# Moving x updates, norm transposes and the first weight unit around the stage boundaries of a two-block transformer kernel

## What is computed

```
x = x + gt_m * (merged @ w_out)                                  # stage out1
x = x + gt_f * swiglu(norm(x)*(1+sc)+sh, w_gate_up, w_down)      # f0
x = x + 0.5 * swiglu(rmsnorm(x), ...)                            # f1
x = x + short_conv(rmsnorm(x), conv_w_in, conv_w, conv_w_out)    # cv, cb, co
x = x + 0.5 * swiglu(rmsnorm(x), ...)                            # f2
shared = kv(rmsnorm(x, kv_norm))                                 # kv
x = x + 0.5 * swiglu(rmsnorm(x), ...)                            # f3
cmp = compress(shared k, v)                                      # xp, cm
x = x + nsa(rmsnorm(x), ...)                                     # qg, gn, nsa, wo
x = x + 0.5 * swiglu(rmsnorm(x), ...)                            # f4
swiglu(h, wgu, wd) = (silu(h @ wg) * (h @ wu)) @ wd              # d_ff 2816
rmsnorm(x, g) = x * rsqrt(mean(x*x) + eps) * g
```

## Time and profile before

| | |
|---|---|
| median of 3 runs | 1701.11 us (1697.21 to 1703.31) |
| profiled execution, own time | 1702.62 us |
| its span in the trace | 1700.8 us |
| PE busy | 1510.3 us, 89% of the span |
| DVE busy | 843.8 us, 50% |
| ACT busy | 690.7 us, 41% |
| share of PE in the chain that ended last | 78% |
| of DVE, ACT, DMA, issue | 9%, 5%, 4%, 3% |

### The profile page before, as it was taken

How to read it: one execution, slowest core, us unless ns; L and a number is a source line. 1 busy time by engine, 2 the same in 40 slices (tenths; PEclk the granted TensorE clock), 3 DMA queues, 4 the chain that set the end, 5 groups by cost and what they waited for, 6 DMA issues and landing times.

```text
span 1700.8 us, 17940 instructions
## 1 busy us (share of the span) xinstructions
PE 1510.3 (89%) x6942; PEld 1203.1 (71%) x6942; DVE 843.8 (50%) x1011; ACT 690.7 (41%) x864; POOL 36.1 (2%) x52
## 2 busy tenths in 40 slices
PE   5979886769998999989889999889997777889998
PEld 2757674658887788867668887668886664568886
DVE  1465572544545454444745545445445346544453
ACT  2334343234343444444344444633433445444342
POOL 0010000000000000000000000100000010000000
PEclk8899997879999999999999999989999777999999
DMA  8654553535565456544545564535555230045562
GB/s 297 204 189 133 198 186 112 173 99 184 187 193 173 153 174 197 178 145 148 173 146 182 191 190 156 160 99 192 185 186 173 79 124 1 4 145 187 185 193 78
DMA packets 187879, 270.10 MB, mean 159 GB/s; under 512 B 8350, under 2 KB 134118, under 8 KB 187816
## 3 DMA queue, kind: packets, MB, share of 16 engines
q1 hardware_dynamic: 186660, 267.08, 48.1%
q10 hardware_dynamic: 996, 1.88, 0.3%
q0 software_dynamic: 160, 0.26, 0.1%
HBM read 268.15 MB, written 1.05 MB: 158 GB/s over the span
## 4 chain that ended last, share of the span: by engine, by line
PE 78%; DVE 9%; ACT 5%; DMA 4%; issue 3%; SPq 0%; POOL 0%; ACTq 0%; DVEq 0%
PE bank L1525 23%; PE bank L1527 23%; PE bank L1526 23%; DVE w_lo_ring L1091 2%; ACT w_hi_ring L797 2%; DMA raw_ring<-in_w_in_dram 2%; PE bank L1549 2%; PE bank L1651 1%; DMA arena<-in_w_mod_dram 1%; PE bank L1619 1%; PE bank L1704 1%; DMA raw_ring<-in_w_br_moba_dram 1%; DVE arena L1376 1%; PE bank L1780 1%; DVE arena L1360 0%
## 5 line engine op out<-in xcount | busy, mean ns | idle before, releaser
L1091 DVE TENSOR_TENSOR w_lo_ring<-raw_ring,w_hi_ring 128x2048 fp32r<-128x2048 f32 (+1 forms) x231 | 525.3, 2277 | 563.1 <-ACT w_hi_ring L1043 371.5
L1525 PE MATMUL bank<-w_hi_ring,h_hi 128*128 128x512 f32 (+2 forms) x1392 | 562.4, 404 | 3.2 <-issue 3.2
L1526 PE MATMUL bank<-w_lo_ring,h_hi 128*128 128x512 f32 (+2 forms) x1392 | 549.6, 395 | 0.0
L1527 PE MATMUL bank<-w_hi_ring,h_lo 128*128 128x512 f32 (+2 forms) x1392 | 549.0, 394 | 0.0
L1043 ACT ACTIVATE w_hi_ring<-raw_ring 128x2048 fp32r<-128x2048 f32 x162 | 310.0, 1916 | 343.4 <-PE bank L1527 343.4
L1525 PEld LDWEIGHTS bank<-w_hi_ring,h_hi 128*128 128x128 f32 x1392 | 271.1, 195 | 65.9 <-issue 13.3
L1527 PEld LDWEIGHTS bank<-w_hi_ring,h_lo 128*128 128x128 f32 x1392 | 269.5, 194 | 56.9
L1526 PEld LDWEIGHTS bank<-w_lo_ring,h_hi 128*128 128x128 f32 x1392 | 270.9, 195 | 51.6
L797 ACT ACTIVATE w_hi_ring<-raw_ring 128x2048 fp32r<-128x2048 f32 (+1 forms) x69 | 128.9, 1875 | 186.5 <-PE bank L1527 118.4
L1525 PE MATMUL bank<-w_hi_ring,f_hi 128*128 128x512 f32 x440 | 171.6, 390 | 7.5 <-DVE f_lo L1484 7.5
L1527 PE MATMUL bank<-w_hi_ring,f_lo 128*128 128x512 f32 x440 | 171.4, 389 | 0.0
(11 more groups left out here) (228 smaller groups left out, 900.2 us busy)
## 6 DMA issues: line engine op xcount, KB each, us to landing
raw_ring<-in_ffn_w_gate_up_dram SPq DMA_DIRECT2D x176, 512.0 KB
raw_ring<-in_ffn_w_down_dram SPq DMA_DIRECT2D x44, 1024.0 KB
raw_ring<-in_w_in_dram SPq DMA_DIRECT2D x22, 1024.0 KB
raw_ring<-in_w_gate_up_dram SPq DMA_DIRECT2D x44, 512.0 KB
raw_ring<-in_w_mod_dram SPq DMA_DIRECT2D x18, 1024.0 KB
raw_ring<-in_w_down_dram SPq DMA_DIRECT2D x11, 1024.0 KB
raw_ring<-in_conv_w_in_dram SPq DMA_DIRECT2D x16, 512.0 KB
arena<-in_w_mod_dram SPq DMA_DIRECT2D x6, 1024.0 KB, 15.3
```

Of the source, the lines that this page charges most:

```text
L1091: dve.tensor_tensor(w_lo[:, u % RING, 0:words], raw[:, r % RING, 0:words], w_hi[:, u % RING, 0:words].bitcast(F32), ALU.subtract).then_inc ...
L1525: pe.matmul(dst, hi, whi, start=start, stop=False)
L1526: pe.matmul(dst, hi, wlo, start=False, stop=False)
L1527: return pe.matmul(dst, lo, whi, start=False, stop=stop)
```

## The change

The change touches six places. I call them by the stages on both sides: f0/f1, f1/cv, co/f2, f2/kv, wo/f4 and f3/xp.

1. In a feed-forward's last step the splits of n1 are issued before the transposed activations are read out, and the low split of n2 after the x updates. The high split of n3 goes behind the next norm's squares. This holds for f0 to f3.
2. The last down product becomes four items `dn`, one for each quarter, and at f0/f1, f1/cv and f2/kv the transposes of groups 0 and 1 stand ahead of the last quarter.
3. The last unit of co and wo is done by row half (`by_tt`), with its own semaphore `half_done`, and groups 0 and 1 stand between the halves.
4. n1 is cut in two: its first two row blocks (`gu`, sub 0, or the first part of kv) stand ahead of groups 2 and 3, and the other two behind them and `square`.

Beginning and end of the other norms (1, 6 and 7) stay.

```diff
+    def ffn(f, stage, norm, then=None, begun=False):
+        body = add("ffn", f=f, stage=stage, norm=norm, unit=len(units) - (2 if begun else 0), begun=begun)
...
+        for q in range(4):
+            if q == 3 and then:
+                plan.extend(tgroup("norm", 2, norm=then))
+            add("dn", of=body, q=q)
+    def norm_rest(n):
+        plan.extend(tgroup("norm", 4, norm=n)[2:])
+        add("square")
+    def begin_glu(stage, norm):
+        u = len(units)
+        units.extend([(stage, 0, 0), (stage, 0, 1)])
+        add("gu", unit=u, sub=0)
+        norm_rest(norm)
+        add("gu", unit=u, sub=1)
+    def lin_out(stage, then):
+        lin(stage, 0, 2)
+        add("lin", stage=stage, chunk=1, part=0, parts=2, unit=len(units))
...
+        add("lin", stage=stage, chunk=1, part=1, parts=2, unit=u, sub=0, subs=2, by_tt=True)
+        add("evac", stage=stage, chunk=1, tt=0)
+        plan.extend(tgroup("norm", 2, norm=then))
+        add("lin", stage=stage, chunk=1, part=1, parts=2, unit=u, sub=1, subs=2, by_tt=True)
+        add("evac", stage=stage, chunk=1, tt=1)
+        add("then split", unit=u)
...
-    ffn(0, "f0", 1)
-    norm(2, True)
-    ffn(1, "f1", 2)
-    norm(3, True)
+    ffn(0, "f0", 1, then=2)
+    begin_glu("f1", 2)
+    ffn(1, "f1", 2, then=3, begun=True)
+    begin_glu("cv", 3)
...
-    for c in range(2):
-        lin("co", c, 2)
-    norm(4, True)
-    ffn(2, "f2", 4)
-    norm(5, True)
-    for c in range(3):
+    lin_out("co", 4)
+    begin_glu("f2", 4)
+    ffn(2, "f2", 4, then=5, begun=True)
+    part("kv", 0, 0, 2, inside=[tgroup("norm", 4, norm=5)[2:] + [dict(kind="square")], []])
+    part("kv", 0, 1, 2)
+    plan.extend(evac("kv", 0))
+    for c in range(1, 3):
...
-    for c in range(2):
-        lin("wo", c, 2)
-    norm(8, True)
-    ffn(4, "f4", 8)
+    lin_out("wo", 8)
+    begin_glu("f4", 8)
+    ffn(4, "f4", 8, begun=True)
...
# ACT, item loop
+                if k in ("square", "xp") and after_norm:
+                    u = after_norm.pop()
+                    split(u, unit_raw[u], u - RING + 1)
# ACT, ffn step
+                        for q in qs[1:] if jb < NJ - 1 else [1]:
+                            next_split(q)
...
+                        if jb == NJ - 1:
+                            next_split(2)
...
+                    u = item["unit"] + 3 * NJ - 1 + RING
+                    if u < len(units):
+                        after_norm.append(u)
# DVE, ffn step and dn
-                            if jb == NJ - 1:
-                                for q in (1, 2):
-                                    next_lo(q)
+                        for q in [1, 2] if 0 < jb < NJ - 1 else [1]:
+                            next_lo(q)
...
+                        after_update.append(u - 1)
                         after_norm.append(u)
+                if k == "dn":
...
+                    update(tt, nb, bank[2 + 2 * tt + nb][:, :], "half" if body["f"] else 1)
+                    if q == 3 and after_update:
+                        u = after_update.pop()
+                        lo_split(u, unit_raw[u])
# PE
+                if k == "gu":
+                    kks = range(2 * item["sub"], 2 * item["sub"] + 2)
...
+                    ins = glu_unit(item["unit"], 0, item["need"], kks=kks)
...
+                if k == "dn":
...
+                    for kk in range(2):
+                        ins = down_product(u, (NJ - 1) % 2, kk, nb, tt, False, kk == 1)
+                    ins.then_inc(sem("d_done" if q < 3 else "unit_used"), 1)
```

More of the change, by code:

```diff
@@ L339, in make_plan @@
             item["pi"] = pi_of[item["stage"], item["chunk"]]
+        if k == "lin" and item.get("by_tt") and item["sub"] == 0:
+            item["half"] = number("half")
         if k == "evac":
             st = item["stage"]
+            if item.get("tt") == 0:
+                item["half"] = count["half"] - 1
             if st not in ("out1", "co", "wo"):
@@ L1084, in _ @@
             tick = Tick(dve, "dve_tick")
[L1086 removed]
+            updates, after_norm, after_update = [0], [], []
             def lo_split(u, r, two=lambda a: 0):
@@ L1233, in _ @@
                     elif st in ("out1", "co", "wo"):
-                        wait_product(dve, st, c)
-                        for tt in range(TT):
+                        for tt in range(TT) if "tt" not in item else [item["tt"]]:
+                            if item.get("tt") == 0:
+                                dve.wait_ge(sem("half_done"), item["half"] + 1)
+                            else:
+                                wait_product(dve, st, c)
                             update(tt, c, b[tt][:, :], 0 if st == "out1" else "one")
@@ new lines, in step @@
+                        next_lo(0)
+                        for tt in range(TT):
+                            dve.wait_ge(sem("sg_ready"), 2 * (item["gi"] + jb) + tt + 1 + two(2))
+                            dve.scalar_tensor_tensor(glu_a[:, tt, :], bank[tt][:, GC:2 * GC], rstd[:, tt:tt + 1] if f else 1.0,
+                                                     glu_s[:, tt, :], ALU.mult, ALU.mult).then_inc(sem("act_ready"), 1)
+                        for q in [1, 2] if 0 < jb < NJ - 1 else [1]:
+                            next_lo(q)
@@ L1504, in _ @@
                             step(first + h, i)
-                    for j in range(first + 2 * turns, NJ + 1):
+                    for j in range(first + 2 * turns, NJ):
                         step(j)
@@ L1527, in three, with glu_unit @@
                 return pe.matmul(dst, lo, whi, start=False, stop=stop)
-            def glu_unit(u, half_, need=None, two=lambda a: 0):
+            def glu_unit(u, half_, need=None, two=lambda a: 0, kks=range(4)):
                 pe.wait_ge(sem("raw_done"), u + 1 + two(3))
-                for kk in range(4):
+                for kk in kks:
                     kt = 4 * half_ + kk
@@ L1588, in _ @@
                     for q, kt in enumerate(kts):
-                        if q * subs // len(kts) != sub:
+                        if "by_tt" not in item and q * subs // len(kts) != sub:
                             continue
@@ L1595, in _ @@
                         wv = [r_[:, u % RING, n * q:n * q + n] for r_ in (w_hi, w_lo)]
-                        for tt in range(TT):
+                        for tt in range(TT) if "by_tt" not in item else [sub]:
                             first_ = q == 0 and (single or part == 0)
```

146 lines of the change are left out of this document (65 added, 81 removed).

## The result

The changed kernel takes 1671.03 us (median of four runs, 1669.25 to 1674.26). The kernel before takes 1701.28 us beside it (four runs, 1697.21 to 1703.31). The medians are 30.3 us apart. The ratio over all these runs is 0.9827 with a 95% interval of 0.9803 to 0.9852, which is 29.4 us less (25.2 to 33.5). The forecast was 1675 us in 1668 to 1685. A second measurement of the same kernel gave 1674.28 against 1699.46 (ratio 0.9843, 0.9814 to 0.9872).

The account below looks back on a forecast made before the run. PE was taken to bound each stage, leaving its boundary waits and half-speed matmuls to gain. Terms 5.9 + 3.0 + 7.1 + 7.4 + 4.3 - 0.7 = 27.0 us less gave 1675 us, range 1668 to 1685.

Parts of the forecast that it names:

- f0/f1: Boundary f0/f1: 5.9 us less, as 7.0 gained with 1.1 given back; bounds 4.2 to 7.0.
- co/f2: Boundary co/f2: all 7.1 us of idle and slow-clock time goes; range 5.4 to 7.1.
- f2/kv: Boundary f2/kv: 4.3 us less (2.7 to 4.4); POOL's 4.9 us of small loads and memsets stay hidden before the squares end.
- wo/f4: Boundary wo/f4: all 7.4 us of idle and slow-clock time goes; range 5.7 to 7.4.
- f3/xp: Boundary f3/xp: 0.7 us lost (0 to 2.3) as DVE's splits end later; PE's wait 9.2 us instead of 8.54.
- six terms: Changes at the six boundaries: 5.9, 3.0, 7.1, 7.4 and 4.3 us gained, 0.7 lost, 27.0 in all.
- The 1.1 us that I gave back there: At f0/f1, glu_a queues on DVE behind two later low splits, making PE wait: 1.1 us of the gain lost.
- Late splits: Rival: later weight splits make PE wait for DVE behind five boundaries, 2 us each, 10 in all: 1685 us; chance 0.08.
- Clock: Rival: waits go but the clock still falls at five boundaries, 1.7 us each, 8.5 in all: 1683.5 us; chance 0.09.
- Loads: Rival: weight loads, started later at boundaries, are the true bound; nothing gained, 19 us lost: 1720 us; chance 0.03.
- Half of it: Rival: DVE's fourth update comes late, so PE waits before groups 2 and 3; half the gain, 1688.5 us; chance 0.04.

## Why the prediction was right

**The bound and the terms.** The step that carried the forecast, that inside a stage PE is the bound and that idle time on PE at a boundary can be taken away one for one, held: six terms, none off by more than 0.2 us, though co/f2 and wo/f4 gave 7.28 and 7.57, a little above the upper ends of 7.1 and 7.4 set for them. Only splits and updates in the new order gave nothing, so without the filling of PE's queue there is no gain. Of the 27.3 us, 7.5 go when n1 is not cut and 3.4 when the row halves are left out; that the filling would do as much without the new order on DVE is not shown, since no run has it.

**f0/f1.** The trace starts this stretch 5.30 us earlier than the one before, so the forecast's times are read with 5.3 taken off. (By the forecast's own times, 568.5 and 561.3, n2 should have ended 7.2 us earlier, not 7.0; it ended 6.9 earlier. In the same way the upper ends add up to 29.0, not 29.1.) Groups 0 and 1 start at 541.69 (forecast 541.7), the fourth update ends at 546.2 (546.2), groups 2 and 3 start at 547.09 (546.8), `glu_a` at 557.77 (557.8). The idle ahead of the first group was 0.24 us, not 0.45, and ahead of `glu_a` 2.09, just under the 2.2 to 2.6 given. The 1.1 us that I gave back there measured 0.93 when the split was moved behind `glu_a`.

**f2/kv.** POOL's small loads and memsets ran from 1035.94 to 1040.88, and rstd's chain began at 1041.75 behind the squares: hidden, with 0.9 us to spare.

**f3/xp.** 9.33 us of wait against 9.2 forecast, 0.79 lost against 0.7.

**The rivals.** *Late splits:* no idle on PE with a low split as releaser at any of the five boundaries. *Clock:* granted 1.00 at all five, and still 1.00 behind the 2.09 us in front of `glu_a`. The rule of the Trainium skill, TensorE: Matmul & The Clock Gate, section "A second HAM failure mode: psum-queue depth-cycling", that frequent short idles are enough to make the clock swing, was hardly put to the test by the changed kernel: at four of the five boundaries there is no idle around the transposes, and at f0/f1 the two that are left, 0.24 and 2.09 us, brought no half speed. The run that puts back one of 2.20 us agrees with it: the clock fell to 0.50. Ahead of the 2.09 us PE had run from 541.69 to 556.3 without idle, ahead of the 2.20 only from 544.03 to 546.5; whether that is the reason is not shown, and the full clock behind the 2.09 us may be in part luck.

*Loads:* the high splits of the costliest group still wait for PE, 320.2 of 322.4 us, and f0/f1's low splits for the high ones. The prediction had only the page, which names one releaser for each group. The full list of releasers for the other high splits, before and after, does have loads in it:

```profile
L797 ACT ACTIVATE w_hi_ring<-raw_ring 128x2048 fp32r<-128x2048 f32 (+1 forms) x69 | 128.9, 1875 | 186.5 <-PE bank L1527 118.4 <-DMA raw_ring<-in_w_in_dram 47.7 <-DMA raw_ring<-in_w_out_dram 11.7
L832 ACT ACTIVATE w_hi_ring<-raw_ring 128x2048 fp32r<-128x2048 f32 (+1 forms) x73 | 136.5, 1876 | 180.8 <-PE bank L1563 113.5 <-DMA raw_ring<-in_w_in_dram 48.1 <-DMA raw_ring<-in_w_out_dram 11.7
```

These are loads of two projections of the first block; the last high split that waits for a load starts at 305 us before and 300 after, ahead of every boundary here. The two waits add up to 59.4 us before and 59.8 after, so the later start of the loads at the boundaries cost nothing.

*Half of it:* the fourth update ended 0.9 us before PE came to groups 2 and 3.

**What was not forecast.** The span fell by 32.8 us and the terms give 27.3. The 5.5 us between them are in untouched work, 5.3 of it ahead of the first boundary. The same instructions up to there took 537.1 and 542.2 us in two executions of the changed kernel, 542.4 and 544.2 in the one before, and 535.1 to 543.3 in the other variants. In the second pair of traces that stretch gives 2.0 and all the rest together 2.1. So the 5.5 can be what one execution differs from another, and the medians, 30.3 and 25.2 us apart in the two measurements, lie on both sides of 27.3. It is not settled: the three longest of the ten, 542.4, 543.3 and 544.2, are the kernel before twice and the one with only the new order of splits, and of the seven others only one comes near, with 542.2. A small part that belongs to the change can't be excluded.

## What to carry to other kernels

At a stage boundary, look for PE's waits behind in-order queues, and ask what independent matmuls could stand in them: part of the next product ahead of the last pieces of the norm filled them here, while reordering the helper engine alone moved the wait from one group of transposes to the next. Price such a wait with the half-speed matmuls that may follow it. And where a boundary's work reads only old data, as the inputs of `cm` do, move it ahead of the whole stage: that took 15.1 us of waits away, over half of what the change itself gave at its six places, and the whole time fell by 21.5.

## What was unexpected of the hardware

Whether a short idle brings the clock down is not settled by its length. Idles of 1.08 and 1.56 us at f2/kv were followed by a clock of 0.50 in one execution of the kernel before, with transposes of 1.92 us; in another, 1.08 and 1.55 were followed by a clock of 1.00 and transposes of 1.44 us; 1.08 and 1.56 at f1/cv brought 1.69 us in that second one, 1.10 and 1.53 brought 1.44 in the first. An idle of 2.09 us left the clock at 1.00, one of 2.20 us brought 0.50. A boundary without idle was the same to 0.1 us in every trace that has it (f1/cv 20.00 to 20.06 us in six). The second price of a wait, the half speed behind it, is thus a chance and not a constant, and a single trace can carry several microseconds of it.
